# A gather of expert rows with TensorE sums: 64x64 tiles, query blocks in pieces, and one table asked for two picks later

## The reference, cut to what matters

```python
q = (xb @ w_pq).reshape(PEER_BLOCK, PEER_HEADS, 2, PEER_DKH)
s = jnp.einsum('thpd,hpkd->thpk', q, sub_keys).astype(jnp.float32)
sv, si = lax.top_k(s, PEER_TOPK)
...
eidx = jnp.take_along_axis(cidx, pos, axis=-1)
g = jax.nn.softmax(best, axis=-1)
act = jax.nn.gelu(jnp.einsum('thkd,td->thk', expert_u[eidx], xb).astype(jnp.float32), approximate=False)
return jnp.einsum('thk,thkd->td', (g * act).astype(xb.dtype), expert_v[eidx])
```

## Time and profile before

| | |
|---|---|
| median of 3 runs | 1871.2 us (1868.68 to 1879.18) |
| the profiled execution | 1862.66 us, of it 1860.9 us from first to last instruction |
| mean granted TensorE clock | 0.915 of full speed |
| busy: PE, PEld, DVE, ACT, POOL | 85%, 52%, 51%, 28%, 31% of the span |
| moved | 438.50 MB, mean 236 GB/s |
| GpSimd asks for `u` rows | from 242.8 to 1001.0 us, 256 times |
| the two indirect DMAs of a pick, GpSimd's time | 0.98 and 0.99 us on average |

### The profile page before, as it was taken

The page is one execution under the profiler, slowest core; times in us unless marked ns, Lnnn a source line. Parts: engine busy times, 40 slices in busy tenths (PEclk is TensorE's granted clock), DMA queues, the critical chain, the costliest instruction groups (busy, mean ns, idle before and its releaser), DMA issues.

```text
span 1860.9 us, 18421 instructions
## 1 busy us (share of the span) xinstructions
PE 1572.5 (85%) x5974; PEld 966.6 (52%) x5974; DVE 955.0 (51%) x2207; ACT 527.7 (28%) x1470; POOL 580.8 (31%) x596
## 2 busy tenths in 40 slices
PE   7998988886758667546646999999999999999998
PEld 2644654343434223212212587677775587677775
DVE  1786666756666666678876346421123246421122
ACT  2244323432223324222322254321112244321111
POOL 0010056655565767677764002100000002100000
PEclk9999999987878788767767999999999999999999
DMA  9864089988897999999999532175442422175410
GB/s 364 317 237 176 1 330 360 364 321 316 328 373 285 379 347 379 354 374 400 398 366 402 180 112 70 49 251 166 158 147 99 150 101 81 39 250 174 159 46 23
DMA packets 170725, 438.50 MB, mean 236 GB/s; under 512 B 12531, under 2 KB 59027, under 8 KB 170500
## 3 DMA queue, kind: packets, MB, share of 16 engines
q0 software_dynamic: 81824, 299.86, 42.7%
q1 hardware_dynamic: 88806, 137.46, 21.2%
HBM read 436.23 MB, written 1.05 MB: 235 GB/s over the span
## 4 chain that ended last, share of the span: by engine, by line
PE 64%; issue 11%; DVE 8%; POOL 8%; ACT 2%; DMA 2%; DVEq 2%; another core or an unknown queue 1%; SPq 0%; ACTq 0%; POOLq 0%
PE psum L1192 15%; PE psum L1203 6%; PE psum L836 5%; PE psum L966 4%; PE psum L837 4%; POOL arena L1339 4%; POOL arena L1334 4%; PE psum L668 4%; DVE arena L2296 3%; PE psum L874 2%; PE psum L1217 2%; PE psum L1180 2%; PE psum L648 2%; PE psum L850 1%; PE psum L992 1%
## 5 line engine op out<-in xcount | busy, mean ns | idle before, releaser
L836 PE MATMUL psum<-arena 128*128 128x512 f32 x382 | 249.5, 740 | 204.7 <-issue 106.6
L2296 DVE CUSTOM_DVE_ANT_0 arena<-arena,psum 128x1024 f32<-128x1024 f32 x224 | 273.6, 1221 | 185.8 <-DMA arena<-in_expert_u,indices 117.8
L1339 POOL DMA_INDIRECT arena<-in_expert_v,indices x256 | 252.8, 988 | 163.0 <-issue 71.8
L1334 POOL DMA_INDIRECT arena<-in_expert_u,indices x256 | 250.6, 979 | 92.8 <-issue 71.2
L1192 PE MATMUL psum<-activations_T,weight_ring 128*128 128x256 f32 x1280 | 279.2, 379 | 0.0
L1192 PEld LDWEIGHTS psum<-activations_T,weight_ring 128*128 128x128 f32 x1280 | 243.0, 190 | 39.8 <-issue 7.6
L836 PEld LDWEIGHTS psum<-arena 128*128 128x128 f32 x382 | 76.9, 226 | 337.3 <-issue 207.3
L2538 DVE SCALAR_TENSOR_TENSOR arena<-psum,small,arena 128x254 f32<-128x254 f32 (+1 forms) x176 | 76.8, 478 | 321.1 <-ACT arena L1797 317.5
L837 PE MATMUL psum<-arena 128*128 128x512 f32 x382 | 231.7, 693 | 0.0
L1288 POOL TENSOR_TENSOR small<-small 128x1 f32<-128x1 f32 (+5 forms) x30 | 30.7, 1024 | 532.6 <-DVE small L2432 194.4
L1614 ACT ACTIVATE activations_T<-activations_T 128x1 f32<-128x1 f32 x256 | 51.1, 200 | 348.0 <-DVE activations_T L2296 185.0
(11 more groups left out here) (408 smaller groups left out, 2052.3 us busy)
## 6 DMA issues: line engine op xcount, KB each, us to landing
weight_ring<-in_ffn_w_in SPq DMA_DIRECT2D x44, 1024.0 KB, 7.8
weight_ring<-in_w_in SPq DMA_DIRECT2D x14, 2048.0 KB, 8.4
arena<-in_ffn_w_out POOLq DMA_DIRECT2D x22, 1024.0 KB, 5.3
weight_ring<-in_w_ada SPq DMA_DIRECT2D x8, 2048.0 KB, 11.5
weight_ring<-in_w_out SPq DMA_DIRECT2D x6, 2048.0 KB, 8.5
weight_ring<-in_w_ada SPq DMA_DIRECT2D x16, 512.0 KB, 9.5
weight_ring<-in_w_pq SPq DMA_DIRECT2D x4, 2048.0 KB, 19.3
weight_ring<-in_w_in SPq DMA_DIRECT2D x2, 2080.0 KB, 21.7
```

The costliest lines, as they stand in the source:

```text
L836: mm(o0, DIAG[:, j % ND, :], VROWS[n % NV][:, 0:512], start=m == 0, stop=last)
L1334: nc.gpsimd.indirect_dma_start(UROWS[g % NU], None, a["expert_u"], bass.IndirectOffsetOnAxis(ap=where, axis=0)).then_inc(sem(f"u_row{g % N ...
L1339: nc.gpsimd.indirect_dma_start(VROWS[g % NV], None, a["expert_v"], bass.IndirectOffsetOnAxis(ap=where, axis=0)).then_inc(sem(f"v_row{g % N ...
L2296: ttr(out=DOTJ[n >= UNIT], in0=UROWS[n % NU], in1=h2, scale=1.0, scalar=0.0, op0=ALU.mult, op1=ALU.add, accum_out=DOT[:, i, m:m + 1]).then ...
```

## The change

It has four parts.

**Sums through four 64x64 tiles.** `DIAG` is diagonal, so tokens 0 to 63 (`TOP`) and 64 to 127 (`BOTTOM`) never mix. The two matmuls of 128x128 become four of 64x64, each with 512 columns: token half times column half. Bank `o0` now holds tokens 0 to 63, their first 512 columns in partitions 0 to 63 and the second in 64 to 127; `o1` holds the other tokens. `gathered` is rewritten for this layout.

**Query blocks in pieces.** `queries` becomes a generator that stops after every four matmuls (eight records). Blocks (0, 2), (0, 3), (1, 0), (1, 1) and (1, 2) have one piece ahead of each of the eight picks up to the place where the whole block stood; (1, 3) has two pieces ahead of each of four; (0, 1) stays whole at pick 1.

**The second table two picks later.** GpSimd asks for the `v` rows of pick g-2 and then for the `u` rows of pick g (`BEHIND` = 2).

```diff
+        TOP, BOTTOM = slice(0, 64), slice(64, P)
+        BEHIND = 2
...
                 for f in range(4):
                     for k in range(KT):
                         ins = mm(o[:, f * P:(f + 1) * P], wpq[b][:, k, f * P:(f + 1) * P], H2T[i][:, k, :], start=k == 0, stop=k == KT - 1)
-                ins.then_inc(a_full, 1)
-                if i == 1:
-                    was_read("a", 3 - b)
-                at["pqt"][i, b] = c["a"]
+                        if k == 3:
+                            yield
+                    if f == 3:
+                        ins.then_inc(a_full, 1)
+                        if i == 1:
+                            was_read("a", 3 - b)
+                        at["pqt"][i, b] = c["a"]
+                    yield
...
-            coming = {1: lambda: queries(0, 1), 6: lambda: scores(0, 1), 20: lambda: queries(0, 2), 27: lambda: scores(0, 2),
-                      34: lambda: h2_turned(1), 42: lambda: queries(0, 3), 50: lambda: scores(0, 3),
+            coming = {6: lambda: scores(0, 1), 27: lambda: scores(0, 2), 34: lambda: h2_turned(1), 50: lambda: scores(0, 3),
                       PICKS - 12: lambda: h2_back(1, bank_a, a_full)}
+            for i, b, last, count in [(0, 1, 1, 1), (0, 2, 20, 8), (0, 3, 42, 8)] + [(1, b, QAT[b], 8 if b < 3 else 4) for b in range(4)]:
+                pieces = queries(i, b)
+                for n in range(last - count + 1, last + 1):
+                    coming[n] = lambda pieces=pieces, count=count: [next(pieces) for _ in range(8 // count)]
...
-                    mm(o0, DIAG[:, j % ND, :], VROWS[n % NV][:, 0:512], start=m == 0, stop=last)
-                    mm(o1, DIAG[:, j % ND, :], VROWS[n % NV][:, 512:1024], start=m == 0, stop=last).then_inc(sem("v_used"), 1)
+                    for half in range(2):
+                        for o, t in ((o0, TOP), (o1, BOTTOM)):
+                            ins = mm(o[(TOP, BOTTOM)[half], :], DIAG[t, j % ND, t], VROWS[n % NV][t, half * 512:(half + 1) * 512], start=m == 0, stop=last)
+                    ins.then_inc(sem("v_used"), 1)
...
+            def v_rows(n):
+
+                if n - NV in added:
+                    pool.wait_ge(sem("v_added"), added[n - NV] + 1)
+                elif n >= NV:
+                    pool.wait_ge(sem("v_used"), summed[n - NV] + 1)
+                nc.gpsimd.indirect_dma_start(VROWS[n % NV], None, a["expert_v"],
+                                             bass.IndirectOffsetOnAxis(ap=EIDX[:, n // PICKS, n % PICKS:n % PICKS + 1], axis=0)).then_inc(sem(f"v_row{n % NV}"), 16)
+
             for g in range(2 * PICKS):
                 i, m = g // PICKS, g % PICKS
+                if g >= BEHIND:
+                    v_rows(g - BEHIND)
...
-                for h in range(2):
-                    e = slice(h * 512, (h + 1) * 512)
-                    o = full()
-                    tt(PROD[:, e], o, MODB[:, 3, e], ALU.mult).then_inc(d_free, 1)
-                    dve.drain()
-                    ins = tt(X[:, i, e], X[:, i, e], PROD[:, e], ALU.add)
-                ins.then_inc(sem("x_ready"), 1)
+                for h in range(2):
+                    e = slice(h * 512, (h + 1) * 512)
+                    for b, t in enumerate((TOP, BOTTOM)):
+                        s = (TOP, BOTTOM)[h]
+                        ins = tt(PROD[t, e], o[b][s, :], MODB[s, 3, e], ALU.mult)
+                        if h == 1:
+                            ins.then_inc(d_free, 1)
+                dve.drain()
+                tt(X[:, i, :], X[:, i, :], PROD, ALU.add).then_inc(sem("x_ready"), 1)
```

## The result

The changed kernel takes 1849.95 us (1848.89 to 1851.65) where the kernel before takes 1872.72 (1868.68 to 1879.18): ratio 0.989, 95% interval [0.986, 0.992], so 1.1% faster. Of the two profiled executions the one of before was the fastest of its runs, 1862.66 us; the one of after took 1849.20. Between these two 13.5 us lie, and these are what the rows can explain. I had predicted 41 less, 1830 as a median. The direction was right, the size was not.

What follows compares the result with a forecast made beforehand. Gather bound by DMA (floor 655 of 761 us) plus GpSimd's waits: 30 and 17 gained, 6 lost, 41 in all. Profile 1862.7 becomes 1821.7, plus 8.5 for the median: 1830 us, own range 1810 to 1848 (50%), overall 1798 to 1890.

Steps and rivals of the forecast that it cites:

- the sum's second term: GpSimd's gather waits that end "remote", for TensorE's signal: half of 33.9 us removed, 17 gained (bounds none, all).
- The later deadline: In the gather, `v` requested later lets TensorE come 3.8 us later before GpSimd stands still; 1.9 used up in steady state.
- Waits for a sum: GpSimd's gather waits for TensorE's sums, mostly behind query blocks: 47.7 us, of which 30 gained.
- Waits for VectorE: GpSimd's gather waits for VectorE grow, as GpSimd standing less meets VectorE's busy stretches: 6 us lost.
- Tiles and switches: TensorE's sums in the gather: 0.95 us per sum with tiles side by side, 0.11 us per change of shape.
- that rival: Tiles don't run at once: a summed pick takes 3.44 us on TensorE in the gather, 26 us slower, 1897; 5%.
- the upper of my bounds: Rewritten `gathered` multiplications on 64 partitions: each takes half to all of 0.69 us; the upper bound is 0.69.
- GpSimd's wait is replaced: In the gather, VectorE's holes and "remote" waits fill the time won; some 12 us remain: 1858, from 1845 to 1868; 17%.
- holes of VectorE: VectorE idle 2.67 us with nothing to wait for while GpSimd asks without pause; such holes may fill the time won.
- The price per instruction: Each added TensorE record in the gather costs up to 0.109 us, 764 records 83 us: +53 net, about 1924; 15%.
- Nothing is left: Shorter sums and split blocks remove all block and "remote" waits in the gather: 70 to 80 us, about 1798; 13%.

Runs made afterwards that it cites:

- delay alone: Kernel before with only the second table two picks later: 0.997 of before with late signals, 1.001 without.
- tiles alone: Kernel before with only the four 64x64 tiles for sums: 1.000 of before with late signals, 1.001 without.
- whole sums, pieces and delay: Changed kernel with whole 128x128 sums, query blocks in pieces and second table two picks later: 0.988 of before with late signals, 1.000 without.
- pieces alone: Kernel before with only the query blocks in pieces: 0.988 of before with late signals, 1.000 without.
- four narrow matmuls: Kernel before with each sum in four matmuls of 256 columns instead of two of 512, first and last picks excepted: 1864.1 us, 1.0035 of before.
- first call: First set of follow-up runs made together, without late signals; the kernel before took 1775.48 us there.
- the pause at each eighth pick: Kernel before with query blocks in pieces; every eighth pick GpSimd waits for `u` rows of two picks earlier: 1855.5 us, 0.993 with late signals; 1846.4, 1.040 without.
- two picks back: Kernel before, but GpSimd asks for a pick's `u` rows only once those of two picks earlier have landed: 1936.1 us, 1.037 of before.
- half rows: Kernel before with requests for 2 KB rows instead of 4 KB, both halves of the work using the same 512 columns: 1859.9 us, 0.994 of before.

## Why the prediction was right or wrong

**The failed step** is the sum's second term: "I take half, 17 gained", of the 33.9 us of "remote" waits. They rose instead, by the same count (without the 0.30 us each that is there anyway) to 65.4 - 36 x 0.30 = 54.6, so 20.7 us were lost: 38 us off, more than the whole miss of 28 between 41 and 13.5. Two things were wrong in it. The later deadline did shorten them, but by 9 us, and what GpSimd gained it stood waiting for VectorE (delay alone). And the tiles, which I had costed by TensorE's time alone, added 24 us (tiles alone), while GpSimd's other waits fell by as much. Without the tiles the 41 would have been missed too: with whole sums, pieces and delay the "remote" waits were 29.2 us, 9 less and not 17, and the ratio was 0.988 again. The prediction's own sign of being wrong, more than thirteen such waits, was met with 36, and its sign of being right, the last `u` request near 960, was not: it starts at 989.9. I had written that a signal which comes only once GpSimd is silent would just move the wait. The row at 423.45 suggests it, but "only" doesn't hold: 15 of the 49 late signals that ScalarE waited for came while GpSimd asked. The pieces alone have 22 "remote" waits for 13, so some of what the blocks' stops had cost came back as waits of the other kind; whether those stops had let signals through is a guess. Why the signals are late stays open.

**Waits for a sum.** Predicted 30 gained; measured 47.7 - (15.4 - 12 x 0.30) = 35.9. Right, and its kind too: under 25 us in total, none of 8. Pieces alone have one of 8.3 left, so tiles and delay helped a little here.

**Waits for VectorE.** Predicted 6 lost; 0.7 gained with all three parts, as the "remote" waits stood in front of them. With pieces and delay and whole sums they were 10 higher, so my 6 would have been near without the tiles.

**GpSimd's own time.** Not in my sum. A `u` request took 1.012 us on average instead of 0.979 in the list of groups, 8 us over 256. The waits of the three kinds are 14.1 us less, the stops that end in "issue" 4.0 less (143.0 us before, 139.0 now); these 18, less the 8, are 10 of the 12.5 us by which the requests' span is shorter, and some 2 stay open.

**Tiles and switches.** Sums are 0.96 us apart where TensorE catches up; 0.95 predicted. The tiles run side by side; that rival is refuted. The halved time of a sum bought nothing in the program's time (tiles alone, 1.000 [0.998, 1.002]): in the rows above GpSimd waits for the signal long after the sum is over.

**`gathered`.** Its four multiplications are one row, 2.81 us, so 0.70 each and the upper of my bounds:

```profile
1004.38 2.81 DVE L2237 TENSOR_TENSOR arena<-psum,arena 64x512 f32<-64x512 f32 x4 [5.41 <-PEq L848]
```

**The rivals.** "GpSimd's wait is replaced" is what happened in part, by "remote" waits, and 1850 lies in its 1845 to 1868; it had 17%. It had the blocks' gain eaten up as a whole, down to 12 us; 35.9 were gained there and 20.7 lost on "remote" waits, so that the time falls into this range is partly luck. Its holes of VectorE were not the cause: GpSimd's waits for VectorE stayed level. The price per instruction was the right place with the wrong size: four tiles and four narrow matmuls both about doubled the "remote" waits (32 and 24 for 13), at 0.000 and 0.009 us a record. "Nothing is left" needed late signals to come from TensorE's long runs; in that case the pieces would have ended them, and 22 stayed.

## What to carry to other kernels

A wait that ends later than the work it waits for can't be costed by that work: read how late the signal is before giving a shorter producer any credit. A stop that is taken away can come back elsewhere: of the 28 us that the delay took from the waits for TensorE, 27 came back as waits for VectorE. When a stop is put in to test something, look at an engine that the stop doesn't touch (ScalarE here), since the stop can hide the wait that it is meant to cure. Run the kernel before in each call and read its own time first: the kernel before and the one with the pieces were 1.2% apart in one call and equal in another.

## What the runs showed of the hardware

In a call with late signals, TensorE's signals can come 12 to 14 us after the sums, four of them within 0.3 us. Many come 1 to 4.4 us after GpSimd's last request, and others (15 of 49 in the changed kernel) while it asks. In such stretches TensorE's own matmuls can come one per 0.71 us (eight from 388.2 to 393.9). Of the 191 sums of the changed kernel 16 took over 2 us from first record to the start of the last; with the tiles alone in the call without late signals none took over 1.0.

Nothing of this was there in two of six calls, on chips that had it in others, with the same kernel: 1775 us against 1858 to 1873. What changes between the calls is not known. Slow packets do not go with it: of the 4 KB packets from 242 to 900 us, 1356 of 55,405 took over 300 ns in the kernel before and 272 of 63,371 with the pieces alone in the first call, but 1560 of 57,616 with the pause at each eighth pick in the other call without late signals, and 2705 of 51,480 with two picks back, which has none either.

Something else does go with it. The traces without late signals hold 13,162 to 13,193 records of semaphore updates in all; the one of two picks back holds 12,228, that of the pause at each eighth pick with late signals 8148, and the others with late signals 6526 to 7606 (before 7315, changed 7287). So where signals come late, up to half of the updates are missing from the trace. Some stops that end in "issue" may therefore be waits whose end was not recorded, and whether signals and records are held up by one thing, perhaps by the profiling itself, no run tells.

A share of bandwidth that something else takes does not explain it alone: the kernel before reaches 409 GB/s over 40 us with late signals too, and half rows at 187 GB/s had as many. The Trainium skill (DMA: Bandwidth & Descriptors, Measured) says that two cores of one HBM domain that both stream get about 358 GB/s each. The means of 360 and 366 look like it beside the 405 of the calls without late signals, and the two rows just named speak against it; that something beside the core uses the memory in some calls is not excluded. Open is also whether the changed kernel as a whole is equal to before without late signals: its parts are, but it was not run there as a whole.
